# Turning the router matmul round: the 36 weight columns stationary, the 128 residual rows moving, in an encoder layer with hierarchical experts

## Chip, cores and metric

One core of one Trainium2 chip runs the whole kernel. The metric is the device time of one execution in microseconds (us); lower is better. Times given are a median of three executions, and one further execution was recorded by the profiler.

## What is computed

One encoder layer on 1024 tokens of width 1024: RMSNorm, one projection, three token mixers (neighbourhood attention, banded sliding-window attention, centred pooling), an output projection and a residual add; then RMSNorm and a hierarchical mixture of experts, a residual add and a final RMSNorm. What matters here is the router: for every token 4 group logits and 32 expert logits, the best group, and the two best experts in it.

```python
def hierarchical_moe(h, rg_w, rg_b, re_w, re_b, e_gate, e_up, e_down):
    t = h.reshape(-1, D)
    g_prob = softmax(t @ rg_w + rg_b)                 # 4 groups
    g_top_p, g_top = lax.top_k(g_prob, 1)
    e_logits = (t @ re_w + re_b).reshape(-1, 4, 8)    # 32 experts
    e_sel = jnp.take_along_axis(e_logits, g_top[:, :, None], axis=1)[:, 0]
    e_top_p, e_top = lax.top_k(softmax(e_sel), 2)
    ...
    for e in range(32):
        y = (silu(t @ e_gate[e]) * (t @ e_up[e])) @ e_down[e]
        out = out + combine[:, e:e + 1] * y
```

## The kernel before

Tokens are cut into TT = 8 tiles of 128 rows. Every engine has its own hand-written instruction list, and semaphores tie the lists together; nothing is reordered by a scheduler. The stages are: projection, mixers, the output projection in two halves of 512 output columns (its last matmul starts at 396.36 us), the router's end (to 411 us), 32 experts (to about 702 us), and the sum over experts with the final norm.

The large matmuls use a split of each fp32 operand into a high and a low part (three matmuls, lines 898 to 900 for the output projection). The router is the exception: its logits decide which expert a token goes to, so `logits(t)` (line 914) multiplies in full fp32. The program prints one instruction for such a matmul; the profile shows two records for it, and one record for a transposition.

The second half of the output projection, `out_proj(1, t)`, carries the router inside it. On TensorE a turn of the loop over t is: the first four k-steps of `out_proj(1, t)` (12 matmuls), the transposition of the second half of the previous tile's residual rows, `x1_transposes(t - 1, 1)`, that of the first half of this tile, `x1_transposes(t, 0)` (line 911), the other four k-steps, and `logits(t - 1)`: eight matmuls with the transposed residual rows `x1T` (128 x 128) stationary and the router weights `rw` (128 x 36) moving (line 925). The result, 128 tokens by 36 logits, lies in PSUM bank 6 or 7 in the form that VectorE wants.

```python
mm = nc.tensor.matmul(ps[:, 6 + t % 2, 0:NR], x1T[t % 2][:, k, :], rw[:, k, :],
                      start=(k == 0), stop=(k == KT - 1))
```

VectorE adds the residual (`residual`, line 1590), scales a tile's logits by the row's 1/rms (`take_logits`, line 1616, which waits for the logits and for `rstd_b`), writes the normalised rows (`normalise2`, line 1594), and copies the first half of the transposed rows from PSUM (`x1T_take`, line 1603). ScalarE sums the squares (`square2`, line 1256) and copies the second half (`x1T_copy`, line 1262); GpSimd makes 1/rms from the sum (line 1983). The ranks of tokens 0 to 511 within their experts are worked out while tiles 5 to 7 are still in the projection: `choose_group(0)`, `choose_first(0)`, `choose_second(0)` on VectorE (the last ends with line 1692), then `rank(0)` on TensorE (line 938).

After the last projection matmul comes the router's end. The logits of tile 6 are made in two halves round the transposition of tile 7's second half, then those of tile 7; VectorE takes them, chooses, ranks (line 938 again) and makes the lists of tokens (lines 956 and 1762); GpSimd gathers the first expert's rows (line 2085), and the experts start. `fill(n)` are matmuls without use that TensorE runs while it waits for VectorE.

In an expert's turn TensorE runs 36 large matmuls and ten transpositions; SyncE fetches the weights of expert e + 4 into the buffers that expert e gives back (`fetch_half`, line 596, waits for a count of TensorE's).

Of the kernel before, what the change touches and what calls it, by code (L numbers as in the profile page):

```python
# [26 lines left out]
F32 = mybir.dt.float32  # L27
# [5 lines left out]
P = 128  # L33
D = 1024
S = 1024
TT = S // P
KT = D // P
# [82 lines left out]
def encoder(nc, x, norm1_g, w_in, nat_tab, swa_sink, pool_w, pool_scale, w_out, norm2_g,  # L120
# [8 lines left out]
    with ExitStack() as ctx:  # L129
# [5 lines left out]
        def at(name, shape, dt, off):  # L135
            return nc.alloc_sbuf_tensor_at(name, shape, dt, offset=base + int(off))

        def sem(name):
            return ctx.enter_context(nc.semaphore(name))
# [111 lines left out]
        xThi = [at(f"xThi{i}", [P, KT, CAP], F32R, TMP + 2560 * i) for i in range(2)]  # L251
        xTlo = [at(f"xTlo{i}", [P, KT, CAP], F32R, (TMP + 5120, W + 53 * KB)[i]) for i in range(2)]
        sg = at("sg", [CAP, DE], F32, TD + 32 * KB)
        hx = at("hx", [COLS, DE], F32, TD + 33 * KB)
        hThi_e = at("hThi_e", [P, 2, CAP], F32R, TD + 34 * KB)
        hTlo_e = at("hTlo_e", [P, 2, CAP], F32R, TD + 34 * KB + 640)
# [71 lines left out]
        x1T_a = sem("x1T_a")  # L328
        x1T_b = sem("x1T_b")
        logit_mm = sem("logit_mm")  # L330
        logit_done = sem("logit_done")
        rd = sem("rd")
        chosen = sem("chosen")
# [362 lines left out]
        def _(pe):  # L696
# [217 lines left out]
            def logits(t, ks=range(KT)):  # L914

                if ks[0] == 0:
                    pe.wait_ge(x1T_a, t + 1)
                    if t >= 2:
                        pe.wait_ge(logit_done, t - 1)
                    if t == TT - 2:  # L920
                        pe.wait_ge(row_hots, 1)
                if ks[-1] >= 4:
                    pe.wait_ge(x1T_b, t + 1)
                for k in ks:
                    mm = nc.tensor.matmul(ps[:, 6 + t % 2, 0:NR], x1T[t % 2][:, k, :], rw[:, k, :],  # L925
                                          start=(k == 0), stop=(k == KT - 1))
                if ks[-1] == KT - 1:
                    mm.then_inc(logit_mm, 1)

            def rank(g):  # L930

# [30 lines left out]
                out_proj(0, t)  # L962
            pe.wait_ge(rw_scaled, 1)
            for t in range(TT):
                out_proj(1, t, range(4))
                if t >= 1:
                    x1_transposes(t - 1, 1)
                x1_transposes(t, 0)
                if t == TT - 2:
                    rank(0)  # L970
                out_proj(1, t, range(4, KT))
                if 1 <= t < TT - 1:
                    logits(t - 1)
            logits(TT - 2, range(4))
            x1_transposes(TT - 1, 1)
            logits(TT - 2, range(4, KT))
            logits(TT - 1)
            lists(0)
            pe.wait_ge(x1_done, 2 * TT)
            fill(FILL_CHOICE)  # L980
# [141 lines left out]
        def _(act):  # L1122
# [135 lines left out]
            def x1T_copy(t):  # L1258
                act.wait_ge(x1tr_b, t + 1)
                if t >= 2:  # L1260
                    act.wait_ge(logit_mm, t - 1)
                nc.scalar.copy(x1T[t % 2][:, 4:8, :], ps[:, 5, :].rearrange("p (c q) -> p c q", c=4)).then_inc(x1T_b, 1)

            for t in range(TT):
                square2(t)
                if t < TT - 1:
                    x1T_copy(t)

            act.wait_ge(rstd_b, TT)
            act.wait_ge(h2_end, 2)  # L1270
# [115 lines left out]
        def _(dve):  # L1386
# [224 lines left out]
                                        gbc[:].rearrange("q (p k) -> q k p", k=KT)[:, :, part], ALU.mult).then_inc(h2_end, 1)  # L1611

            def take_logits(t):
                dve.wait_ge(logit_mm, t + 1)
                dve.wait_ge(rstd_b, t + 1)
                nc.vector.scalar_tensor_tensor(out=logit[:, t, :], in0=ps[:, 6 + t % 2, 0:NR],
                                               scalar=stat[:, 3, t:t + 1], in1=rb[:], op0=ALU.mult, op1=ALU.add).then_inc(logit_done, 1)

            count = [0]
# [99 lines left out]
                v.tensor_reduce(ek[:, 2 * TG * g:2 * TG * (g + 1)], mine, AX_X, ALU.add)  # L1719

            nc.vector.memset(hx[:], 0.0).then_inc(zeroed, 1)
            dve.wait_ge(g_in, 32)
            for g in range(TT):
                residual(g)
# [469 lines left out]
```

## Time and profile before

| what | us |
|---|---|
| median of 3 executions | 737.96 (737.53 to 738.65) |
| the profiled execution, its own time | 738.25 |
| its span (first to last recorded instruction) | 736.4 |
| TensorE busy with matmuls | 707.0 (96%) |
| VectorE busy | 513.5 (70%) |
| ScalarE busy | 391.3 (53%) |
| GpSimd busy | 321.9 (44%) |
| granted TensorE clock, mean over the span | 0.996 of full speed |

The profile is of one execution. Its sections are: busy time of each engine, the span in 40 slices, DMA queues, the chain of work that ended last, and groups of instructions with what they waited for. PE is TensorE's matmuls, PEld its weight loads, DVE VectorE, ACT ScalarE, POOL GpSimd, SPq SyncE's DMA queue. The ends of matmuls are modelled, so the duration of one contains time in which the next already runs; distances between starts are measured.

### The profile page before, as it was taken

To read this page: it belongs to the slowest core of one execution; us is meant where nothing else is said; L and a number is where in the kernel's file an instruction comes from. 1 tells how busy PE (TensorE), PEld (TensorE's weight loads), DVE (VectorE), ACT (ScalarE), POOL (GpSimd) and SP (SyncE) were. 2 spreads that over 40 slices of the span, in tenths; PEclk is the share of its full clock that TensorE was granted. 3 is DMA by queue.
4 is the path that set the end of the run, shared out by engine and by line. 5 is a ranking of instruction groups with operands and counts; after the bars stand their busy time and mean duration, and the time that the engine had idled before them with its cause. 6 is when DMAs were issued, how large, how long until landed. Compare 5 with 4: busy or idle time off the path is not lost.

```text
span 736.4 us, 10256 instructions
## 1 busy us (share of the span) xinstructions
PE 707.0 (96%) x3757; PEld 510.2 (69%) x3757; DVE 513.5 (70%) x811; ACT 391.3 (53%) x585; POOL 321.9 (44%) x241
## 2 busy tenths in 40 slices
PE   7999999999999999999999899999999999999983
PEld 7888888886665445888889666666666666666631
DVE  5646422216887877513487888888888888888977
ACT  6500001104777778201123478888888888887815
POOL 1523458944677774440010254444444444442213
PEclk9999999999999999999999999999999999999998
DMA  9422112101400001905646499999999999999979
GB/s 305 139 58 58 30 56 58 29 0 36 109 1 1 1 1 38 289 17 201 225 160 251 139 335 387 391 384 380 382 388 383 390 387 385 383 383 381 399 270 357
DMA packets 62419, 157.74 MB, mean 214 GB/s; under 512 B 10168, under 2 KB 24992, under 8 KB 62368
## 3 DMA queue, kind: packets, MB, share of 16 engines
q1 hardware_dynamic: 55728, 139.58, 52.7%
q0 software_dynamic: 6336, 16.89, 6.8%
q8 instruction: 31, 0.51, 0.3%
q10 hardware_dynamic: 304, 0.59, 0.2%
q14 instruction: 20, 0.16, 0.1%
HBM read 142.36 MB, written 18.87 MB: 219 GB/s over the span
## 4 chain that ended last, share of the span: by engine, by line
PE 86%; DVE 5%; DMA 3%; issue 2%; ACT 2%; POOL 2%; DVEq 0%; SPq 0%; POOLq 0%
PE ps L1015 8%; PE ps L1020 8%; PE ps L1023 8%; PE ps L733 6%; PE ps L734 6%; PE ps L732 6%; PE ps L898 4%; PE ps L1046 4%; PE ps L1042 4%; PE ps L900 4%; PE ps L1050 4%; PE ps L899 4%; PE ps L836 3%; PE ps L991 2%; PE ps L925 2%
## 5 line engine op out<-in xcount | busy, mean ns | idle before, releaser
L1818 DVE TENSOR_TENSOR wgulo<-wgu,unit 128x2048 fp32r<-128x2048 f32 x64 | 146.3, 2287 | 26.1 <-ACT unit L1283 26.0
L1283 ACT CAST unit<-wgu 128x2048 fp32r<-128x2048 f32 x64 | 122.4, 1912 | 2.4 <-DVE eid L1779 1.1
L2092 POOL DMA_INDIRECT expert_rows<-ysb,idx x32 | 71.1, 2221 | 107.1 <-ACT ysb L1330 106.1
L2085 POOL DMA_INDIRECT xg<-h_rows,idx x32 | 59.1, 1847 | 71.6 <-PE ps L991 58.9
L732 PE MATMUL ps<-hThi,whi 128*128 128x512 f32 x200 | 78.3, 392 | 0.0
L734 PE MATMUL ps<-hThi,wlo 128*128 128x512 f32 x200 | 77.9, 389 | 0.0
L733 PE MATMUL ps<-hTlo,whi 128*128 128x512 f32 x200 | 77.8, 389 | 0.0
L1824 DVE TENSOR_TENSOR wdlo<-wd,unit 128x2048 fp32r<-128x2048 f32 x32 | 73.1, 2285 | 2.5 <-ACT unit L1292 2.5
L1015 PE MATMUL ps<-unit,xThi 128*80 128x512 f32 x256 | 70.8, 398 | 0.8 <-ACT xThi L1307 0.8
L1020 PE MATMUL ps<-unit,xTlo 128*80 128x512 f32 x256 | 69.2, 391 | 0.0
L1023 PE MATMUL ps<-wgulo,xThi 128*80 128x512 f32 x256 | 69.1, 391 | 0.0
L2047 POOL TENSOR_SCALAR pswa<-pswa,esum 128x384 f32<-128x384 f32 (+1 forms) x48 | 56.6, 1194 | 18.8 <-DVE esum L1540 18.8
L1292 ACT CAST unit<-wd 128x2048 fp32r<-128x2048 f32 x32 | 61.1, 1910 | 4.4 <-DMA wd<-in_expert_w_down 4.4
L1144 ACT COPY kb<-ps 64x512 f32<-64x512 f32 x8 | 4.7, 583 | 92.6 <-DVE ps L1417 92.5
L1020 PEld LDWEIGHTS ps<-unit,xTlo 128*80 128x80 f32 x256 | 37.8, 148 | 21.1 <-DVE xTlo L1831 0.2
L1023 PEld LDWEIGHTS ps<-wgulo,xThi 128*80 128x80 f32 x256 | 37.8, 148 | 21.1
L898 PE MATMUL ps<-wohi,oThi 128*128 128x512 f32 x128 | 51.3, 401 | 0.0
L900 PE MATMUL ps<-wohi,oTlo 128*128 128x512 f32 x128 | 50.0, 391 | 0.0
L899 PE MATMUL ps<-wolo,oThi 128*128 128x512 f32 x128 | 49.9, 390 | 0.0
L1184 ACT ACTIVATE pswa<-pswa,mneg 128x385 f32<-128x385 f32 (+1 forms) x64 | 37.5, 588 | 18.2 <-DVE mneg L1533 18.0
L1015 PEld LDWEIGHTS ps<-unit,xThi 128*80 128x80 f32 x256 | 35.4, 148 | 16.7 <-ACT xThi L1307 0.9
L1980 POOL TENSOR_SCALAR stat<-stat 128x1 f32<-128x1 f32 x16 | 5.5, 343 | 88.1 <-ACT h L1256 64.4
(226 smaller groups left out, 1453.4 us busy)
## 6 DMA issues: line engine op xcount, KB each, us to landing
wgu<-in_expert_w_gate SPq DMA_DIRECT2D x64, 512.0 KB, 13.0
wgu<-in_expert_w_up SPq DMA_DIRECT2D x64, 512.0 KB, 15.7
wd<-in_expert_w_down SPq DMA_DIRECT2D x32, 1024.0 KB, 18.0
y<-expert_rows SPq DMA_DIRECT2D x16, 512.0 KB, 10.4
wraw<-in_w_in SPq DMA_DIRECT2D x14, 512.0 KB, 3.9
xin<-in_x SPq DMA_DIRECT2D x8, 512.0 KB, 6.7
x<-in_x SPq DMA_DIRECT2D x8, 512.0 KB, 7.5
out<-fo SPq DMA_DIRECT2D x8, 512.0 KB, 3.8
```

The costliest lines, as they stand in the source:

```text
L732: nc.tensor.matmul(bank, whi[i % 2][:, k, :], hThi[:, k, cols], start=(k == 0), stop=False)
L733: nc.tensor.matmul(bank, whi[i % 2][:, k, :], hTlo[:, k, cols], start=False, stop=False)
L734: mm = nc.tensor.matmul(bank, wlo[i % 2][:, k, :], hThi[:, k, cols], start=False, stop=(k == KT - 1))
L898: nc.tensor.matmul(ps[:, g % 4, :], oThi[t][:, k, :], wohi[n][:, k, :], start=(k == 0), stop=False)
L899: nc.tensor.matmul(ps[:, g % 4, :], oThi[t][:, k, :], wolo[n][:, k, :], start=False, stop=False)
L900: mm = nc.tensor.matmul(ps[:, g % 4, :], oTlo[t][:, k, :], wohi[n][:, k, :], start=False, stop=(k == KT - 1))
L1015: nc.tensor.matmul(bank, xThi[e % 2][:, 4 * a + k, :], hi[:, :, k * DE:(k + 1) * DE], start=(a == 0 and k == 0), stop=False)
L1020: nc.tensor.matmul(bank, xTlo[e % 2][:, 4 * a + k, :], hi[:, :, k * DE:(k + 1) * DE], start=False, stop=False)
L1023: mm = nc.tensor.matmul(bank, xThi[e % 2][:, 4 * a + k, :], lo[:, :, k * DE:(k + 1) * DE], start=False, stop=(a == 1 and k == 3))
L1283: nc.scalar.copy(weight_unit(e, a)[:], raw_half(wgu, e, a)).then_inc(ahi_done, 1)
L1818: nc.vector.tensor_tensor(raw_half(wgulo, e, a), raw_half(wgu, e, a), weight_unit(e, a)[:].bitcast(F32), ALU.subtract).then_inc(alo_done, 1)
L1824: nc.vector.tensor_tensor(wdlo[e % RING][:].rearrange("p j d -> p (j d)").rearrange("p (a f) -> p a f", a=2), wd[e % RING][:].rearrange("p ...
```

## The change

The operands of the router matmul change places: `rw[:, k, :]` (36 columns) is stationary and `x1T` (128 columns) moves, so the product is 36 logits by 128 tokens, on 36 partitions. ScalarE copies it to a 128 x 128 buffer in SBUF, whose other 92 rows VectorE has set to zero once (`lt`, two buffers), and TensorE transposes that buffer back into columns 128 to 255 of the same PSUM bank, from which VectorE takes it. In the stream the transposition of tile t - 2 stands behind the first k-step of `out_proj(1, t)`. At the end the logits of tile 6 are no longer split round the transposition of tile 7's rows. Line numbers below are those of the changed kernel in the order listings; 898 to 900 became 902 to 904, 911 became 915, 925 became 929.

```diff
--- before.py
+++ after.py
@@ -251,6 +251,7 @@
         xThi = [at(f"xThi{i}", [P, KT, CAP], F32R, TMP + 2560 * i) for i in range(2)]
         xTlo = [at(f"xTlo{i}", [P, KT, CAP], F32R, (TMP + 5120, W + 53 * KB)[i]) for i in range(2)]
         sg = at("sg", [CAP, DE], F32, TD + 32 * KB)
+        lt = [at(f"lt{i}", [P, P], F32, TD + 32 * KB + 512 * i) for i in range(2)]
         hx = at("hx", [COLS, DE], F32, TD + 33 * KB)
         hThi_e = at("hThi_e", [P, 2, CAP], F32R, TD + 34 * KB)
         hTlo_e = at("hTlo_e", [P, 2, CAP], F32R, TD + 34 * KB + 640)
@@ -328,6 +329,9 @@
         x1T_a = sem("x1T_a")
         x1T_b = sem("x1T_b")
         logit_mm = sem("logit_mm")
+        lt_zeroed = sem("lt_zeroed")
+        lt_copied = sem("lt_copied")
+        logit_turned = sem("logit_turned")
         logit_done = sem("logit_done")
         rd = sem("rd")
         chosen = sem("chosen")
@@ -922,10 +926,15 @@
                 if ks[-1] >= 4:
                     pe.wait_ge(x1T_b, t + 1)
                 for k in ks:
-                    mm = nc.tensor.matmul(ps[:, 6 + t % 2, 0:NR], x1T[t % 2][:, k, :], rw[:, k, :],
+                    mm = nc.tensor.matmul(ps[0:NR, 6 + t % 2, 0:P], rw[:, k, :], x1T[t % 2][:, k, :],
                                           start=(k == 0), stop=(k == KT - 1))
                 if ks[-1] == KT - 1:
                     mm.then_inc(logit_mm, 1)
+
+            def logits_turned(t):
+
+                pe.wait_ge(lt_copied, t + 1)
+                nc.tensor.transpose(ps[:, 6 + t % 2, P:2 * P], lt[t % 2][:], ident[:]).then_inc(logit_turned, 1)
 
             def rank(g):
 
@@ -962,7 +971,10 @@
                 out_proj(0, t)
             pe.wait_ge(rw_scaled, 1)
             for t in range(TT):
-                out_proj(1, t, range(4))
+                out_proj(1, t, range(1))
+                if t >= 2:
+                    logits_turned(t - 2)
+                out_proj(1, t, range(1, 4))
                 if t >= 1:
                     x1_transposes(t - 1, 1)
                 x1_transposes(t, 0)
@@ -971,10 +983,11 @@
                 out_proj(1, t, range(4, KT))
                 if 1 <= t < TT - 1:
                     logits(t - 1)
-            logits(TT - 2, range(4))
+            logits(TT - 2)
             x1_transposes(TT - 1, 1)
-            logits(TT - 2, range(4, KT))
+            logits_turned(TT - 2)
             logits(TT - 1)
+            logits_turned(TT - 1)
             lists(0)
             pe.wait_ge(x1_done, 2 * TT)
             fill(FILL_CHOICE)
@@ -1261,10 +1274,21 @@
                     act.wait_ge(logit_mm, t - 1)
                 nc.scalar.copy(x1T[t % 2][:, 4:8, :], ps[:, 5, :].rearrange("p (c q) -> p c q", c=4)).then_inc(x1T_b, 1)
 
+            def lt_copy(t):
+                act.wait_ge(logit_mm, t + 1)
+                if t == 0:
+                    act.wait_ge(lt_zeroed, 2)
+                if t >= 2:
+                    act.wait_ge(logit_turned, t - 1)
+                nc.scalar.copy(lt[t % 2][0:NR, :], ps[0:NR, 6 + t % 2, 0:P]).then_inc(lt_copied, 1)
+
             for t in range(TT):
+                if t >= 1:
+                    lt_copy(t - 1)
                 square2(t)
                 if t < TT - 1:
                     x1T_copy(t)
+            lt_copy(TT - 1)
 
             act.wait_ge(rstd_b, TT)
             act.wait_ge(h2_end, 2)
@@ -1611,9 +1635,9 @@
                                         gbc[:].rearrange("q (p k) -> q k p", k=KT)[:, :, part], ALU.mult).then_inc(h2_end, 1)
 
             def take_logits(t):
-                dve.wait_ge(logit_mm, t + 1)
+                dve.wait_ge(logit_turned, t + 1)
                 dve.wait_ge(rstd_b, t + 1)
-                nc.vector.scalar_tensor_tensor(out=logit[:, t, :], in0=ps[:, 6 + t % 2, 0:NR],
+                nc.vector.scalar_tensor_tensor(out=logit[:, t, :], in0=ps[:, 6 + t % 2, P:P + NR],
                                                scalar=stat[:, 3, t:t + 1], in1=rb[:], op0=ALU.mult, op1=ALU.add).then_inc(logit_done, 1)
 
             count = [0]
@@ -1719,6 +1743,8 @@
                 v.tensor_reduce(ek[:, 2 * TG * g:2 * TG * (g + 1)], mine, AX_X, ALU.add)
 
             nc.vector.memset(hx[:], 0.0).then_inc(zeroed, 1)
+            for i in range(2):
+                nc.vector.memset(lt[i][:], 0.0).then_inc(lt_zeroed, 1)
             dve.wait_ge(g_in, 32)
             for g in range(TT):
                 residual(g)
```

The end of the router stage on TensorE, before (`ident,x` is the transposition of residual rows, `rw,x1T` the logits, `tile_hot,row_hot` the first lists):

```order
L900 MATMUL ps<-wohi_149,oTlo_147 128x512
L925 MATMUL ps<-rw,x1T_167 128x36 [waits row_hots,logit_done,x1T_a]
L925 MATMUL ps<-rw,x1T_167 128x36 x3
L911 MATMUL ps<-ident,x_164 128x128 [waits x1T_b,x1_done]
L911 MATMUL ps<-ident,x_164 128x128 x3
L925 MATMUL ps<-rw,x1T_167 128x36 [waits x1T_b]
L925 MATMUL ps<-rw,x1T_167 128x36 x3
L925 MATMUL ps<-rw,x1T_168 128x36 [waits x1T_b,logit_done,x1T_a]
L925 MATMUL ps<-rw,x1T_168 128x36 x7
L956 MATMUL ps<-tile_hot_175,row_hot_173 80x64 [waits row_hots]
```

and after the change (`ident,lt` is the transposition back):

```order
L902 MATMUL ps<-wohi_149,oThi_139 128x512
L903 MATMUL ps<-wolo_151,oThi_139 128x512
L904 MATMUL ps<-wohi_149,oTlo_147 128x512
L929 MATMUL ps<-x1T_167,rw 36x128 [waits row_hots,x1T_b,logit_done,x1T_a]
L929 MATMUL ps<-x1T_167,rw 36x128 x7
L915 MATMUL ps<-ident,x_164 128x128 [waits x1T_b,x1_done]
L915 MATMUL ps<-ident,x_164 128x128 x3
L937 MATMUL ps<-ident,lt_219 128x128 [waits lt_copied]
L929 MATMUL ps<-x1T_168,rw 36x128 [waits x1T_b,logit_done,x1T_a]
L929 MATMUL ps<-x1T_168,rw 36x128 x7
L937 MATMUL ps<-ident,lt_220 128x128 [waits lt_copied]
L965 MATMUL ps<-tile_hot_175,row_hot_173 80x64 [waits row_hots]
```

All eight matmuls of tile 6 now stand ahead of the transposition of tile 7's rows; one transposition back, which waits for ScalarE, stands between the two tiles' logits and one behind them.

In the stream, from the logits of tile 5 to the first k-steps of tile 7's projection, the changed TensorE list reads:

```order
L929 MATMUL ps<-x1T_168,rw 36x128 [waits x1T_b,logit_done,x1T_a]
L929 MATMUL ps<-x1T_168,rw 36x128 x7
L902 MATMUL ps<-wohi_149,oThi_139 128x512 [waits x1_done,pool_out,oTlo_done]
L903 MATMUL ps<-wolo_151,oThi_139 128x512
L904 MATMUL ps<-wohi_149,oTlo_147 128x512
L937 MATMUL ps<-ident,lt_220 128x128 [waits lt_copied]
L902 MATMUL ps<-wohi_149,oThi_139 128x512 [waits x1_done,pool_out,oTlo_done]
L903 MATMUL ps<-wolo_151,oThi_139 128x512
L904 MATMUL ps<-wohi_149,oTlo_147 128x512
```

One transposition is set behind the first three projection matmuls, and a second set of the projection's waits behind it.

ScalarE's list over tiles 6 and 7 now (`ACTIVATE` sums the squares of a tile, the last one with its junk output in `ps`):

```order
L1283 COPY lt_220<-ps 36x128 [waits logit_turned,logit_mm]
L1269 ACTIVATE h_165,stat<-x_164 128x1024 [waits h2_stored0,x1_done]
L1275 COPY x1T_167<-ps 128x512 [waits logit_mm,x1tr_b]
L1283 COPY lt_219<-ps 36x128 [waits logit_turned,logit_mm]
L1269 ACTIVATE ps,stat<-x_164 128x1024 [waits x1_done]
L1283 COPY lt_220<-ps 36x128 [waits logit_turned,logit_mm]
L1295 ACTIVATE h_166<-h_166,stat 128x1024 [waits h2_end,rstd_b]
```

The copy of a tile's logits stands ahead of the next tile's sum of squares, and the last copy ahead of the last scaling.

## Rows read from the trace of the kernel before

**Rows 1.** page, part 4: shares of the chain that ended last, by engine.

```profile
PE 86%; DVE 5%; DMA 3%; issue 2%; ACT 2%; POOL 2%; DVEq 0%; SPq 0%; POOLq 0%
```

**Rows 2.** busy time by stretch (us; records), granted clock, DMA share, GB/s.

```profile
337.00:396.40 59.40, 59.40 (x346) 51.48 (x344) 34.95 (x60) 12.05 (x21) 5.68 (x14) 1.00 0.59 214
...
440.00:700.00 260.00, 259.97 (x1329) 173.57 (x1328) 231.49 (x182) 217.13 (x203) 113.83 (x56) 1.00 1.03 385
```

**Rows 3.** who waited for whom on SyncE's DMA queue, 330 to 736 us.

```profile
SPq L596 <- PE ps L1023: 104.6, 47, 3.5
```

**Rows 4.** TensorE in order of time, one tile: start us, us, line, shapes, records.

```profile
388.18 0.39 PE L900 MATMUL ps<-wohi,oTlo 128*128 128x512 f32 x1
388.41 1.87 PE L925 MATMUL ps<-rw,x1T 128*128 128x36 f32 x16
...
390.43 0.39 PE L899 MATMUL ps<-wolo,oThi 128*128 128x512 f32 x1
...
392.97 1.03 PE L911 MATMUL ps<-ident,x 128*128 128x128 f32 x8
...
394.07 0.39 PE L899 MATMUL ps<-wolo,oThi 128*128 128x512 f32 x1
```

**Rows 5.** TensorE in order of time, two other full-precision groups.

```profile
215.85 1.09 PE L854 MATMUL ps<-ptna,vtok 128*64 128x128 f32 x16
...
409.44 1.36 PE L956 MATMUL ps<-tile_hot,row_hot 128*80 128x64 f32 x16 [0.92 <-DVE row_hot L1710]
```

**Rows 6.** groups of TensorE instructions by form: busy us, mean ns, idle before.

```profile
L866 PE MATMUL ps<-cu,pwd 128*128 128x512 f32 x8 | 3.7, 605 | 0.0
```

**Rows 7.** order of time, engines around tile 6's second half.

```profile
389.41 1.06 ACT L1256 ACTIVATE h<-x 128x1024 f32<-128x1024 f32 x1 [4.31 <-DVE x L1590]
...
390.94 0.57 POOL L1983 TENSOR_TENSOR stat<-stat,neg_half 128x1 f32<-128x1 f32 x1
...
392.13 2.19 DVE L1594 SCALAR_TENSOR_TENSOR h<-x,stat,gbc 128x1024 f32<-128x1024 f32 x1
```

**Rows 8.** order of time: VectorE's choice for tiles 0 to 3, TensorE's ranks.

```profile
381.23 0.26 DVE L1616 SCALAR_TENSOR_TENSOR logit<-ps,stat,rb 128x36 f32<-128x36 f32 x1 [0.29 <-PE ps L925]
...
382.73 0.29 DVE L1692 TENSOR_TENSOR rt<-rs 128x128 f32<-128x128 f32 x1
...
384.75 0.39 PE L938 MATMUL ps<-rt,ut 128*128 128x128 f32 x2
```

**Rows 9.** groups of ScalarE instructions by form, two small ones.

```profile
L1298 ACT ACTIVATE rs<-rs 128x32 f32<-128x32 f32 x1 | 0.2, 229 | 2.1 <-DVE rt L1692 2.1
...
L1315 ACT CAST hThi_e<-ps 128x160 fp32r<-128x160 f32 x2 | 0.6, 292 | 0.0
```

**Rows 10.** order of time, all engines, end of the router stage.

```profile
396.36 0.39 PE L900 MATMUL ps<-wohi,oTlo 128*128 128x512 f32 x1
...
396.59 0.97 PE L925 MATMUL ps<-rw,x1T 128*128 128x36 f32 x8
...
396.79 0.69 DVE L1590 TENSOR_TENSOR x<-ps,x 128x512 f32<-128x512 f32 x1 [0.74 <-PE ps L900]
...
397.52 1.03 ACT L1256 ACTIVATE ps<-x 128x1024 f32<-128x1024 f32 x1 [3.33 <-DVE x L1590]
...
397.54 0.66 PE L911 MATMUL ps<-ident,x 128*128 128x128 f32 x4
...
398.03 2.98 PE L925 MATMUL ps<-rw,x1T 128*128 128x36 f32 x24
...
398.23 0.69 DVE L1603 COPY x1T<-ps 128x512 f32<-128x512 f32 x1 [0.75 <-PE ps L911]
...
399.05 0.56 POOL L1983 TENSOR_TENSOR stat<-stat,neg_half 128x1 f32<-128x1 f32 x1
...
401.05 0.25 DVE L1616 SCALAR_TENSOR_TENSOR logit<-ps,stat,rb 128x36 f32<-128x36 f32 x1 [0.75 <-PE ps L925]
```

**Rows 11.** order of time: the token lists, then the first gather.

```profile
410.84 0.22 DVE L1762 TENSOR_SCALAR idx<-ps 80x64 int32<-80x64 f32 x1
```

## The prediction

> **What bounds the kernel now.** I read the chain that ended last first. TensorE carries 86% of it and VectorE 5% [rows 1], so an edit counts where it lengthens TensorE's list or one of the few places where TensorE waits for somebody. Then the stretches [rows 2]. While the router's logits are made inside the output projection (337 to 396 us), matmuls cover the whole time at a granted clock of 1.00, the 2.4 GHz level: there TensorE is the bound, and whatever its list gains or loses goes straight into the time. In the experts' stage (440 to 700 us) matmuls again cover everything, but the DMA engines are full too, with 385 GB/s. Who waits for whom decides there: SyncE's fetches wait 104.6 us in sum for TensorE's matmuls [rows 3], so the weights follow TensorE and a late start of the stage should be a late end. Between the two lies the router's end, from the last projection matmul at 396.36 to the first gather, ordered by a chain through TensorE and VectorE [rows 10, 11]. The change touches the stream and this end, so the forecast is two sums.
>
> **The matmuls themselves.** The cost of a group is the distance between projection matmuls on its two sides less that of one projection matmul. Ordinary distance: 388.41 - 388.18 = 0.23 us. For a tile's logits, 390.43 - 388.41 = 2.02 us, less 0.23, is 1.79 us for 16 records (eight matmuls of two), 0.112 each; for eight transpositions 394.07 - 392.97 = 1.10, less 0.23, is 0.87, 0.109 each, and the last record's own length is 1.03 - 7 x 0.109 = 0.27 [rows 4]. What sets 0.112 is the load of 128 stationary columns, not the 36 moving ones: a group with 80 stationary and 64 moving columns needs (1.36 - 0.27)/15 = 0.073 a record [rows 5]. From 128 to 80 columns that is 0.039 less, so 36 columns load in about 0.04, an estimate from these two groups. Then the 128 moving columns are the limit. Their price is not shown for this shape. From above it is the present 0.112. From below stands a group with 64 stationary and 128 moving columns, (1.09 - 0.27)/15 = 0.055 [rows 5]; but by `times_values` its heads alternate between the lower and the upper half of the output partitions. The group with 128 stationary and 512 moving columns does not alternate: (3.7 - 0.605)/7 = 0.44 a record, 0.11 for a quarter of the columns [rows 6]. The router's output lies on the same 36 partitions throughout, so I take the value of the rows that do not alternate, 0.109. A tile's logits then cost 16 x 0.109 = 1.75 us and save 0.04.
>
> The Trainium skill says otherwise at one place and the same at another. Its page "TensorE: Matmul & The Clock Gate", section "Back-to-back issue gap", gives an isolated gap of N/2.4 + 2.5 ns, 56 ns for 128 moving columns; by that the sum would be the fast rival's below, and the transpositions at 0.109 don't fit it. Its page "FP8 and Floating Point Precision", section "TensorE Precision Notes", says that true fp32 takes four passes through the array; four times 128 columns at 2.4 GHz are 213 ns a matmul, which agrees with two records of 0.109 and speaks against this change, because the passes now run over 128 columns instead of 36.
>
> **In the stream.** Six transpositions back (tiles 0 to 5) are new TensorE work at 0.11 each [rows 4]. With the 0.04 saved per tile, TensorE's stream grows by 6 x (0.11 - 0.04) = 0.42 us. Do they wait? ScalarE's copy can start when the last logit record has ended, 0.27 after its start; it moves 128 elements per partition, between 0.229 for 32 and 0.292 for 160 [rows 9], so I take 0.29. With two handovers of 0.04 it is ready 0.64 after the last record's start; three projection matmuls behind that record take the list to about 0.11 + 3 x 0.23 = 0.80. That fits by some 0.15. The extra semaphore waits of the cut projection call cost nothing as long as TensorE's queue runs ahead; without that cover they are six times some hundredths.
>
> Behind the copy on ScalarE's list stands the sum of squares of the next tile. It began at 389.41, and must now wait for the logits' end (390.29) and the copy: about 390.6, 1.2 later. GpSimd's root then ends at 391.51 + 1.2 = 392.7, and VectorE's normalisation, which began at 392.13, slips to 392.8 or so [rows 7]. VectorE had 0.74 idle before its last residual [rows 10]; this is what is late next, and it is covered. VectorE's logits of tile 4 come behind the turned tile, 381.23 becoming about 382.1, so the choice that ended at 382.73 + 0.29 = 383.02 ends at 383.9; TensorE's ranks that need it start at 384.75 [rows 8]. Nothing there stops TensorE. The two zeroings are two 128 x 128 writes (0.29 each, the row of that width in [rows 8]) on VectorE before the first residual, while TensorE is in the projection's first half; should that cover fail, 0.6 in all.
>
> **At the end.** Count from T, the start of the last projection matmul (396.36). Before, VectorE took tile 7's logits at 401.05, T + 4.69 [rows 10]. The order was: half of tile 6's logits, transposition of tile 7's rows as soon as the residual was added, then the second half of tile 6's logits while VectorE copied the rows out (398.23 to 398.92), then tile 7's logits without a gap (24 records in one row of 2.98). Now all of tile 6's logits come first: they start at T + 0.23 and take 1.75, to T + 1.98. The four transpositions take 0.66, to 2.64. VectorE's copy takes 0.03 + 0.69, to 3.36, with only one transposition back on TensorE meanwhile; tile 7's logits wait for it. 0.03, then 16 x 0.109 + 0.27 = 2.01 bring T + 5.40. ScalarE's copy, 0.03 + 0.29, to 5.72. The transposition back from idle: four took 0.66, so one takes 0.66 - 3 x 0.109 = 0.33, plus 0.04, to 6.09. VectorE's take begins at T + 6.13, 1.44 later than before. Of this about 0.7 is the lost cover of the rows' copy and 0.75 the turn itself. ScalarE's last sum of squares (397.52 before) now begins at about T + 2.4 + 0.42, or 399.2, and 1/rms, which was ready at 399.61, is there about 1.7 later, before it is wanted [rows 10]. The lists, fills and choice behind keep their order, so the delay passes to the lists' end at 410.84 and the first gather at 411.97 [rows 11].
>
> Sum: 0.42 + 1.44 = +1.86 us. Against the profiled execution's 738.25 that is 740.1; the median shown is 0.29 lower, so 739.8. Bounds: with the shortest copy (0.23) and turn (0.27), and no cost of the order beyond the copy itself, +1.2; with a bubble of 0.15 at each turn and the logits at 0.112, +3.1.
>
> **Rivals.**
> Faster: the moving columns go at the alternating group's rate, 0.055 a record [rows 5]. A tile's logits cost 0.87 instead of 1.79, the stream loses 6 x (0.92 - 0.11) = 4.9 us, and at the end tile 6's logits hide behind the residual: transpositions to T + 1.8, copy to 2.5, logits 1.15 to 3.7, turn 0.73 to 4.4, 0.3 earlier. Together -5.2, or 732.8. It decides as soon as a record is below about 0.095, where 128 records save over 1.9. Against it stand the transpositions and the 512-column group. Chance 0.10.
>
> No change: the experts' stage is held by the weights, DMA being full there [rows 2], and the late start is absorbed while fetches for the first experts are in flight; only the stream or less is left, 0 to +0.5, 738.2. Against it, SyncE waits for TensorE and not the reverse [rows 3]. Chance 0.20.
>
> Slower still: the margin of 0.15 at each turn is not there, because the turned tile's load cannot run ahead of its wait; six bubbles of 0.3 are 1.8 more, 741.6. Chance 0.17.
>
> **How the numbers follow.** My forecast, 739.8, has 0.53. The measurement can tell about 0.2%, 1.5 us, from no change, so "slower" begins at 739.4; of my forecast's share 0.10 lies below that (its lower bound is 739.2). Slower: 0.43 + 0.17 = 0.60. Same: 0.20 + 0.10 = 0.30. Faster: 0.10. The range leaves out the fast rival and the upper tail: 738.0 to 741.7.
>
> **What would show it.** The logit groups at 1.75 between their neighbours, with LDWEIGHTS short; VectorE's take of the last logits 1.9 us later on the clock; a wait of about 0.7 before tile 7's logits for VectorE's copy; the first gather at about 413.8, and the experts' end moved by as much. A logit group under 1.5 us makes the forecast wrong on one side; idle TensorE before each turned tile, on the other; an expert stage that is shorter than before would mean that the start was absorbed.

## The result, and the profile after

| | before | changed |
|---|---|---|
| median of 4 executions, us | 737.98 | 742.61 |
| ratio, with its 95% interval | | 1.0064 (1.0049 to 1.0078) |
| span of the profiled execution, us | 736.4 | 741.0 |
| TensorE busy, us | 707.0 | 710.1 |
| VectorE, ScalarE, GpSimd busy, us | 513.5, 391.3, 321.9 | 513.6, 392.5, 322.5 |

The change makes the kernel 4.6 us slower. I had forecast slower, by 1.9 us, with a range to 741.7; the measured time lies above it.

The page's chain that ended last, by engine, for the changed kernel (before: [rows 1]):

```profile
PE 83%; DVE 6%; DMA 5%; ACT 2%; issue 2%; POOL 1%; SPq 1%; DVEq 0%; POOLq 0%
```

TensorE has lost 3% of the span in this chain to VectorE and DMA. Three anchors tell where the time went. The output projection, both halves, runs from its first record (line 898, now 902) to T, the start of the last one: 290.7 to 396.36 before, 290.4 to 398.61 now, 105.66 and 108.17 us. VectorE takes tile 7's logits at T + 4.69 before, at T + 6.34 now. From that take to the token lists it is 9.79 us in both. So 2.51 us came in the stream and 1.65 at the end. The remaining 0.5 is a balance, mainly of 0.7 more in the experts' stage and 0.3 less ahead of the projection. It is treated below.

TensorE in order of time round the logits of tile 5, changed kernel (start us, us, line, shapes, records), which answers to [rows 4]:

```profile
390.02 0.39 PE L904 MATMUL ps<-wohi,oTlo 128*128 128x512 f32 x1
390.34 1.94 PE L929 MATMUL ps<-x1T,rw 128*36 128x128 f32 x16
...
392.55 0.40 PE L903 MATMUL ps<-wolo,oThi 128*128 128x512 f32 x1
392.79 0.39 PE L904 MATMUL ps<-wohi,oTlo 128*128 128x512 f32 x1
393.02 0.27 PE L937 MATMUL ps<-ident,lt 128*128 128x128 f32 x1
...
393.36 0.39 PE L903 MATMUL ps<-wolo,oThi 128*128 128x512 f32 x1
```

A seam, below, is a place where the shape of the stationary operand changes, from 128 columns to 36 or back. Read the distance from the last projection record ahead of the group to the second one behind it, and take off two ordinary distances, 0.46: 392.55 - 390.02 - 0.46 = 2.07 us. Before it was 390.43 - 388.18 - 0.46 = 1.79 [rows 4]; I had put 1.75. The logits of a tile became 0.28 dearer instead of 0.04 cheaper. The transposition back (line 937) costs 393.36 - 392.79 - 0.46 = 0.11, as forecast. Look at the start of the group: the first router record begins 0.32 behind the last projection record, where 0.23 is usual.

The view of line 929, its weight loads, and what they waited for:

```profile
L929 PEld LDWEIGHTS ps<-x1T,rw x128: 109/113/113, 346.5 to 403.9; 128*36 128x36 f32 x128
...
  issue: 3.4, 8
  DVE x1T L1627: 0.8, 1
```

A load of 36 columns now lasts 0.113 us instead of 0.19, so the loads are short, as said. But eight times, once for each group, they had stood idle with "issue" as the reason: nothing that the profile shows held them. Before, this line had no such wait. (One of the eight, at tile 7, falls together with the wait for VectorE; with 65 columns, below, only that one is left.) The 0.8 is the wait for VectorE's copy of tile 7's rows that I had put at 0.7.

All engines at the end of the router stage, changed kernel, which answers to [rows 10] and [rows 11]:

```profile
398.61 0.39 PE L904 MATMUL ps<-wohi,oTlo 128*128 128x512 f32 x1
...
398.93 1.94 PE L929 MATMUL ps<-x1T,rw 128*36 128x128 f32 x16
...
400.79 0.66 PE L915 MATMUL ps<-ident,x 128*128 128x128 f32 x4
400.90 0.26 ACT L1283 COPY lt<-ps 36x128 f32<-36x128 f32 x1 [4.46 <-PE ps L929]
...
401.49 0.69 DVE L1627 COPY x1T<-ps 128x512 f32<-128x512 f32 x1 [1.76 <-PE ps L915]
...
402.32 1.91 PE L929 MATMUL ps<-x1T,rw 128*36 128x128 f32 x16 [0.77 <-DVE x1T L1627]
...
404.27 0.26 ACT L1283 COPY lt<-ps 36x128 f32<-36x128 f32 x1 [2.06 <-PE ps L929]
...
404.58 0.33 PE L937 MATMUL ps<-ident,lt 128*128 128x128 f32 x1 [0.35 <-ACT lt L1283]
...
404.95 0.25 DVE L1640 SCALAR_TENSOR_TENSOR logit<-ps,stat,rb 128x36 f32<-128x36 f32 x1 [1.61 <-PE ps L937]
...
414.74 0.22 DVE L1788 TENSOR_SCALAR idx<-ps 80x64 int32<-80x64 f32 x1
```

Tile 6's logits at T + 0.32, transposition of tile 7's rows at T + 2.18, VectorE's copy to T + 3.57, tile 7's logits from T + 3.71 to T + 5.62, ScalarE's copy, the turn, VectorE's take. The order is the forecast one. The first group and its two seams put the transposition 0.20 behind the forecast T + 1.98. From VectorE's copy to tile 7's logits it is 0.14 instead of the 0.03 of my sum, so they start 0.32 late. And they last 1.91 us, where my sum had 16 x 0.109 + 0.27 = 2.01: one record too many, for by my own reading of such a group it is 15 x 0.109 + 0.27 = 1.91. So the take is 0.21 late. Two errors of 0.11 cancel in this, which was luck.

### The profile page after: what moved, and what is told of

The parts are those of the page before. It is cut to its first block, busy times and chain, and to the rows that moved or that the text cites. A ratio compares the mean times of both kernels' runs of the same rounds, so it can differ in the third digit from the quotient of the medians.

```text
span 741.0 us, 10299 instructions
## 1 busy us (share of the span) xinstructions
PE 710.1 (96%) x3765; PEld 509.0 (69%) x3765; DVE 513.6 (69%) x813; ACT 392.5 (53%) x593; POOL 322.5 (44%) x241
## 4 chain that ended last, share of the span: by engine, by line
PE 83%; DVE 6%; DMA 5%; ACT 2%; issue 2%; POOL 1%; SPq 1%; DVEq 0%; POOLq 0%
PE ps L1028 7%; PE ps L1033 7%; PE ps L1036 7%; PE ps L737 6%; PE ps L738 6%; PE ps L736 6%; PE ps L902 4%; PE ps L904 4%; PE ps L903 4%; PE ps L1059 4%; PE ps L1063 4%; PE ps L1055 4%; PE ps L840 3%; DMA wd<-in_expert_w_down 3%; PE ps L1004 2%; PE ps L929 2%
```

## The experiments

The theories that I set against each other after this profile: (A) TensorE loads a 36-column operand only when it has finished with 128-column ones, and the reverse; (B) the bubble belongs to the short load; (C) it belongs to which operand moves. The table has what came out. Each ratio is against executions of the kernel before that were taken together with that run; the other columns are from one profile each.

| run | ratio to before (95%) | stream, us | take of tile 7 | lists after the take |
|---|---|---|---|---|
| before | 1 | 105.66 | T + 4.69 | 9.79 |
| changed | 1.0064 (1.0049 to 1.0078) | 108.17 | T + 6.34 | 9.79 |
| w64 | 1.0047 (1.0030 to 1.0064) | 108.06 | T + 6.38 | 9.79 |
| w65 | 1.0029 (1.0018 to 1.0040) | 106.15 | T + 6.11 | 9.77 |
| tail_only | 1.0009 (0.9995 to 1.0022) | 105.66 | T + 5.43 | 9.78 |
| dummy36 | 1.0047 (1.0030 to 1.0064) | 109.58 | T + 4.69 | 10.02 |
| dummy80 | 1.0041 (1.0022 to 1.0060) | 107.32 | T + 5.09 | 11.24 |
| w65_split | 1.0030 (1.0019 to 1.0041) | 106.21 | T + 5.85 | 9.78 |
| halves | 0.9974 (0.9965 to 0.9984) | 103.62 | T + 4.77 | 9.79 |
| halves_b | 0.9986 (0.9975 to 0.9997) | 103.58 | T + 4.77 | 9.78 |
| halves_tail | 0.9985 (0.9973 to 0.9996) | 103.60 | T + 4.99 | 10.43 |
| halves_raw | 0.9976 (0.9963 to 0.9989) | 103.58 | T + 4.56 | 9.79 |
| after_b | 1.0061 (1.0048 to 1.0074) | 108.17 | T + 6.34 | 9.79 |

"Stream" runs from the first projection record to T, the take is VectorE's take of tile 7's logits, and the last column is the time from it to the token lists (before: line 1762).

**One column more.** In both kernels the router weights and the router bias behind them are one buffer `rww`, so that a stationary operand can be read wider than 36 columns; what the extra columns give lands on partitions that nobody reads.

```diff
-mm = nc.tensor.matmul(ps[0:NR, 6 + t % 2, 0:P], rw[:, k, :], x1T[t % 2][:, k, :],
+mm = nc.tensor.matmul(ps[0:64, 6 + t % 2, 0:P], rww[:, k * NR:k * NR + 64], x1T[t % 2][:, k, :],
```

> The changed kernel, but the stationary operand of a router matmul is 64 columns wide instead of 36 (the 28 extra columns are the next weights in SBUF; their products go to PSUM partitions that nobody reads). Theory A (between a stationary operand of at most 64 columns and one of more, TensorE does not load ahead: it finishes the one kind before it loads the other, about 0.32 us per group of logits on both sides together): as the changed kernel, 742.6 us (within 1), and from one projection record to the next across a group of logits 2.5 us, against 2.25 in the kernel before. Rival B (the bubble comes with how much the number of columns changes, or from the load being short): smaller than at 36, about 2.35 us, total 741 to 742. Rival C (it comes from which operand moves, whatever the width): 2.5 us, as A; the run with 65 columns tells them apart.

The same with 65 in place of 64:

> As before with 65 columns, one more. Theory A: 65 columns use the full width as the projection's 128 do, the weights are loaded ahead again, and a group of logits takes 16 x 0.109 = 1.75 us, so 2.0 us from projection record to projection record; six groups in the stream save 6 x 0.3 and the two at the end 0.3 to 0.5: 740.3 us (739.9 to 740.8). Rival B: no difference to 64 columns. Rival C: no difference either, 742.6 us.

TensorE in order of time round a group of logits, w64:

```profile
389.06 0.39 PE L905 MATMUL ps<-wohi,oTlo 128*128 128x512 f32 x1
389.38 1.96 PE L930 MATMUL ps<-x1T,rww 128*64 128x128 f32 x16
...
391.61 0.40 PE L904 MATMUL ps<-wolo,oThi 128*128 128x512 f32 x1
```

and w65:

```profile
388.21 0.40 PE L905 MATMUL ps<-wohi,oTlo 128*128 128x512 f32 x1
388.44 1.91 PE L930 MATMUL ps<-x1T,rww 128*65 128x128 f32 x16
...
390.42 0.40 PE L904 MATMUL ps<-wolo,oThi 128*128 128x512 f32 x1
```

With 64 columns the group costs 391.61 - 389.06 - 0.46 = 2.09 us, with 65 columns 390.42 - 388.21 - 0.46 = 1.75, the value of the prediction. One column more saves 0.34 us a group; the stream falls from 108.06 to 106.15, which is 0.49 above before where my sum had 0.42. The bubble is neither graded by the number of columns nor bound to the operand that moves: it comes between 64 and 65. The first weight load of each of these two groups (w64, then w65) shows what it is:

```profile
389.38 1.72 PEld L930 LDWEIGHTS ps<-x1T,rww 128*64 128x64 f32 x16 [0.35 <-issue]
```

```profile
388.21 1.90 PEld L930 LDWEIGHTS ps<-x1T,rww 128*65 128x65 f32 x16
```

With 65 columns it begins together with the last projection matmul, 0.23 ahead of its own matmul; with 64 it begins 0.32 behind that projection matmul, together with its own. At the end w65 takes tile 7's logits at T + 6.11 (prediction: T + 6.13).

**The order at the end alone.** The kernel before, with this edit:

```diff
-            logits(TT - 2, range(4))
+            logits(TT - 2)
             x1_transposes(TT - 1, 1)
-            logits(TT - 2, range(4, KT))
```

> The kernel before, with the changed kernel's order at the end alone: all eight logit matmuls of tile 6 ahead of the transposition of tile 7's rows. My prediction's term: VectorE takes tile 7's logits 0.7 us later (T + 5.4 instead of T + 4.7, T the start of the last projection record), total 738.7 us (738.4 to 739.0). Rival: the order costs nothing, since the residual of tile 7 is late anyhow: T + 4.8, 738.0 us.

```profile
396.43 0.39 PE L900 MATMUL ps<-wohi,oTlo 128*128 128x512 f32 x1
...
399.87 1.95 PE L925 MATMUL ps<-rw,x1T 128*128 128x36 f32 x16 [0.88 <-DVE x1T L1602]
...
401.85 0.26 DVE L1615 SCALAR_TENSOR_TENSOR logit<-ps,stat,rb 128x36 f32<-128x36 f32 x1 [0.97 <-PE ps L925]
```

(In order of time: T, tile 7's logits, VectorE's take of them.) The logits of tile 7 waited 0.88 for VectorE's copy, and the take came at T + 5.43, 0.74 later. The total, 1.0009 with an interval that holds 1, can't tell this from nothing; the trace can.

**A change of width by itself.** The kernel before, its router untouched, with seven useless matmuls in the projection's stream:

```diff
             for t in range(TT):
-                out_proj(1, t, range(4))
+                out_proj(1, t, range(2))
+                if t < TT - 1:
+                    if t >= 3:
+                        pe.wait_ge(logit_done, t - 2)
+                    nc.tensor.matmul(ps[0:36, 6 + (t + 1) % 2, 256:384], ident[:, 0:36], ones[:], start=True, stop=True)
+                out_proj(1, t, range(2, 4))
```

> The kernel before, with one useless full-precision matmul (36 stationary columns of the identity, 128 moving, two records) after the second k-step of the projection in tiles 0 to 6 of the second half. Theory A: each costs its two records, 0.22, plus the two changes of width, 0.3: 0.52 us, 7 x 0.52 = 3.6, total 741.6 us. Rivals B and C (bubble from the group of logits itself: its waits, its moving operand in fresh SBUF): 0.22 each, 739.5 us.

and with 80 in place of 36 in the added line:

> The kernel before with the same seven useless matmuls as in the run with 36 columns, but with 80 stationary columns. Theory A (the full width is used from 65 columns on, no change of width): 0.22 us each for two records, the projection 7 x 0.22 = 1.6 us longer, total 1.6 us above before. Rival (any extra matmul of another kind in the projection's stream costs 0.5): 3.9 us longer, as with 36 columns.

TensorE round one of them, dummy36:

```profile
366.85 0.40 PE L900 MATMUL ps<-wohi,oTlo 128*128 128x512 f32 x1
367.17 0.41 PE L969 MATMUL ps<-ones,ident 128*36 128x128 f32 x2
...
367.85 0.39 PE L899 MATMUL ps<-wolo,oThi 128*128 128x512 f32 x1
```

and dummy80:

```profile
366.21 0.39 PE L900 MATMUL ps<-wohi,oTlo 128*128 128x512 f32 x1
366.44 0.38 PE L969 MATMUL ps<-ones,ident 128*80 128x128 f32 x2
...
366.89 0.40 PE L899 MATMUL ps<-wolo,oThi 128*128 128x512 f32 x1
```

With 36 columns it costs 367.85 - 366.85 - 0.46 = 0.54 us, with 80 columns 366.89 - 366.21 - 0.46 = 0.22, its two records. The difference, 0.32, is the price of going from 128 columns to 36 and back, and it is the same for these two records as for a group of 16. The streams say the same: 3.92 and 1.66 longer, 0.56 and 0.24 each.

The total of dummy80 missed what I expected (1.6 us above before; it was about 3). Busy time by stretch, with the granted clock in the third column from the end, dummy80:

```profile
397.00:402.00 5.00, 4.94 (x40) 4.66 (x38) 2.63 (x4) 1.78 (x3) 0.77 (x2) 0.94 0.65 184
402.00:406.00 4.00, 4.00 (x26) 4.00 (x27) 3.12 (x18) 1.91 (x2) 0.00 (x0) 0.50 0.99 376
```

From 402 to 406 us, at the router's end, the clock was granted at 0.50, that is 1.2 GHz, and the lists came 11.24 us after the take instead of 9.79. The fall began before the take: the 24 logit records behind the last transposition lasted 3.39 us instead of 2.98, which is why the take came at T + 5.09 and not T + 4.69. It isn't the price of 80 columns, for in dummy36 the clock of the same stretch was 0.69, and the lists came 10.02 after the take. In the other profiles it was 1.00, but for halves_tail below. What pulled it down I can't say: in both runs matmul records follow each other without a gap there.

**What is left when the change of width is gone.** w65 with the old order at the end:

```diff
+            logits(TT - 2, range(4))
-            logits(TT - 2)
             x1_transposes(TT - 1, 1)
+            logits(TT - 2, range(4, KT))
             logits_turned(TT - 2)
             logits(TT - 1)
             logits_turned(TT - 1)
```

> The changed kernel with 65 stationary columns and with the old order at the end (half of tile 6's logits, transposition of tile 7's rows, the other half, tile 7's logits). What is left of the change is then the six transpositions back in the stream and the turn at the end. Theory: stream +0.5, and VectorE takes tile 7's logits at T + 5.4 instead of T + 6.1 and T + 4.7 before; total 1.2 us above before (0.9 to 1.6). Rival: VectorE's take of the last logits waits for the rows' 1/rms, which GpSimd has late because ScalarE's sum of squares stands behind the copy of tile 6's logits: then T + 5.4 to 6.0 and up to 1.8 above before.

```profile
399.50 0.33 PE L938 MATMUL ps<-ident,lt 128*128 128x128 f32 x1 [0.35 <-ACT lt L1285]
...
402.29 0.25 DVE L1642 SCALAR_TENSOR_TENSOR logit<-ps,stat,rww 128x36 f32<-128x36 f32 x1 [1.16 <-PE ps L938]
```

(the turn of tile 6, and VectorE's take of tile 7's logits.) The take came at T + 5.85, not T + 5.4: TensorE stood 0.35 us ahead of tile 6's turn, waiting for ScalarE's copy, and tile 7's logits stood behind it in the list. Neither my theory nor the rival (1/rms was ready before the take) had this wait. The total missed too: 0.3% above before, some 2.2 us, where I expected 1.2 (0.9 to 1.6).

**The two halves of the array at once.** If up to 64 columns use half of the array's width, two such matmuls can run side by side, as the attention's values do at 0.055 a record [rows 5]. The even k-steps of the router go to partitions 0 to 63, the odd ones to 64 to 127; the turn adds the halves.

```diff
-mm = nc.tensor.matmul(ps[0:NR, 6 + t % 2, 0:P], rw[:, k, :], x1T[t % 2][:, k, :],
-                      start=(k == 0), stop=(k == KT - 1))
+mm = nc.tensor.matmul(ps[64 * (k % 2):64 * (k % 2) + 64, 6 + t % 2, 0:P], rww[:, k * NR:k * NR + 64], x1T[t % 2][:, k, :],
+                      start=(k < 2), stop=(k >= KT - 2), skip_group_check=True)
...
-nc.tensor.transpose(ps[:, 6 + t % 2, P:2 * P], lt[t % 2][:], ident[:])
+nc.tensor.matmul(ps[:, 6 + t % 2, P:P + NR], lt[t % 2][:], stk[:], start=True, stop=True)
...
-nc.scalar.copy(lt[t % 2][0:NR, :], ps[0:NR, 6 + t % 2, 0:P])
+nc.scalar.copy(lt[t % 2][:], ps[:, 6 + t % 2, 0:P])
...
+nc.vector.tensor_tensor(stk[:], ident[:, 0:NR], ident[:, 64:64 + NR], ALU.add)
```

> The changed kernel, with the router's even k-steps into PSUM partitions 0 to 63 and the odd ones into 64 to 127 (64 stationary columns each), and one full-precision matmul against two stacked identities in place of the transposition back, which turns and adds the two halves. Theory (as with the attention's values, two records of different halves run at once, 0.109 a pair; changes of width cost 0.32 a group; the turn is two records, 0.22): a group of logits takes 0.87 + 0.32 instead of 1.79, the stream is 6 x (0.60 - 0.22) = 2.3 us shorter than before, VectorE takes tile 7's logits at T + 4.8; total 2.2 us below before. Rival (two halves do not overlap when both read the same kind of operand from 128 rows): 16 x 0.109 + 0.32, the stream 3 us longer than before, total 5 us above.

TensorE round a group of logits and a turn (line 941), halves:

```profile
385.15 0.39 PE L906 MATMUL ps<-wohi,oTlo 128*128 128x512 f32 x1
385.46 1.09 PE L931 MATMUL ps<-x1T,rww 128*64 128x128 f32 x16
...
386.83 0.40 PE L905 MATMUL ps<-wolo,oThi 128*128 128x512 f32 x1
387.06 0.40 PE L906 MATMUL ps<-wohi,oTlo 128*128 128x512 f32 x1
387.30 0.31 PE L941 MATMUL ps<-stk,lt 128*128 128x36 f32 x2
...
387.75 0.39 PE L905 MATMUL ps<-wolo,oThi 128*128 128x512 f32 x1
```

The 16 records last 1.09 us together, (1.09 - 0.27)/15 = 0.055 each; the group costs 386.83 - 385.15 - 0.46 = 1.22 with its two changes of width, the turn 387.75 - 387.06 - 0.46 = 0.23. The stream is 2.04 us shorter than before and the take at T + 4.77, both within 0.3 of the expectation. This version is faster than both kernels: 0.9974 of before (0.9965 to 0.9984). Repeated:

> The run halves again, on the chip of the other two: 2.2 us below before (1.3 to 2.9), T + 4.8, lists 9.8 us after the take.

0.9986 (0.9975 to 0.9997), with the same anchors. The gain is there both times, 1.9 and 1.0 us; the second is below the 1.3 at which my range began.

**Its end in another order.**

```diff
             logits(TT - 2)
             x1_transposes(TT - 1, 1)
+            logits(TT - 1, range(4))
+            logits(TT - 1, range(4, KT))
             logits_turned(TT - 2)
-            logits(TT - 1)
             logits_turned(TT - 1)
```

> The same, with another order at the end: tile 6's logits, transposition of tile 7's rows, the first half of tile 7's logits under VectorE's copy of the rows, the second half, then both turns. Theory: VectorE takes tile 7's logits at T + 4.4 to 4.5, 0.3 to 0.4 earlier than without it; total 2.5 us below before. Rival: the take is then held by 1/rms (square sum behind the copy of tile 6's logits), T + 4.7 or later and no gain over the run without it.

VectorE at the end, halves_tail (take of tile 6's logits, the last part of the raw rows, take of tile 7's):

```profile
396.95 0.26 DVE L1643 SCALAR_TENSOR_TENSOR logit<-ps,stat,rww 128x36 f32<-128x36 f32 x1 [1.09 <-PE ps L941]
397.13 1.08 DVE L1636 TENSOR_TENSOR h<-x,gbc 128x512 f32<-128x512 f32 x1
...
398.13 0.25 DVE L1643 SCALAR_TENSOR_TENSOR logit<-ps,stat,rww 128x36 f32<-128x36 f32 x1
```

The take of tile 7's logits stood behind a 1.08 us instruction of VectorE's own, and came at T + 4.99: a miss, with a cause that I had not listed. And the lists came 10.43 behind it. In total the run is 1.1 us below before, not 2.5. Busy time by stretch:

```profile
401.50:403.30 1.80, 0.00 (x0) 0.00 (x0) 1.59 (x11) 0.35 (x2) 0.00 (x0) 1.00 0.70 275
403.30:405.50 2.20, 2.18 (x12) 2.19 (x13) 1.26 (x5) 0.23 (x1) 0.00 (x0) 0.61 0.05 19
```

TensorE had no work for 1.8 us (no record in the first stretch), and its clock fell to 0.61 as a mean of the next. The last run moves that VectorE instruction ahead of the two takes:

```diff
             x1T_take(TT - 1, 1)
-            take_logits(TT - 2)
             last_raw(1)
+            take_logits(TT - 2)
             take_logits(TT - 1)
```

> The run halves_tail, with VectorE's last part of the raw rows (1.08 us) moved ahead of its take of tile 6's logits, into the time in which it waited. Theory: the take of tile 7's logits no longer stands behind it and comes at T + 4.3 instead of T + 5.0, the choice is ready 0.7 earlier, TensorE's idle stretch ahead of the ranks shrinks from 1.8 to 1.1 us, its clock stays at the full level, and the lists come 9.8 us after the take instead of 10.4; total 2.6 us below before. Rival: the drop of the granted clock in that stretch has nothing to do with the idle time; then the lists stay 10.4 us after the take and the total is at most 2.0 below before.

```profile
398.38 0.56 POOL L2011 TENSOR_TENSOR stat<-stat,neg_half 128x1 f32<-128x1 f32 x1
...
399.04 0.25 DVE L1643 SCALAR_TENSOR_TENSOR logit<-ps,stat,rww 128x36 f32<-128x36 f32 x1 [0.49 <-POOL stat L2011]
```

(GpSimd's root, VectorE's take.) TensorE's stretch without a record shrank from 1.84 to 1.41 us, the clock stayed at 1.00 and the lists came 9.79 behind the take again. One profile each shows the idle stretch and the clock going together; dummy36 and dummy80 show that the clock can fall without one. The take itself came at T + 4.56, not T + 4.3: 1/rms of tile 7 was ready only at 398.94, T + 4.47, and VectorE took at once. In halves_tail it was ready at T + 3.72, with ScalarE's list in the same order, so this is not the rival of halves_tail (the square sum behind the copy) but came with the move itself:

```profile
397.12 1.09 DVE L1636 TENSOR_TENSOR h<-x,gbc 128x512 f32<-128x512 f32 x1
...
397.33 0.96 POOL L2008 TENSOR_SCALAR stat<-stat 128x1 f32<-128x1 f32 x1 [6.95 <-ACT ps L1274]
```

GpSimd's step ahead of the root lasted 0.96 us and ended 0.08 behind VectorE's instruction; in halves_tail, where that one came later, it lasted 0.22. The total is 0.9976 (0.9963 to 0.9989), no better than halves within the intervals.

**The changed kernel again.**

> The changed kernel again, on the chip of the other two: projection 2.5 us longer than before, take at T + 6.3; total 4.2 us above before (3.7 to 5.0). If the 0.7 us that its experts' stage was longer in the first profile was no chance, the stage is again 288.7 us or more against 288.1.

It repeats to 0.01 us in the stream and at the end, and 1.0061 in total. Its experts' stage, from the first gate record to the last down record, was 289.5 us, after 288.8 in the first profile and 288.1 in that of before (there from 417.5 to 705.6, so somewhat later than the 702 given above). By the mark that I had set (288.7 or more) that is no chance. But this stage, whose code none of the edits touches, lies between 288.0 (tail_only) and 289.5 over all profiles; 288.2 in w64, which has the whole change in it, and 289.1 in dummy80, which has none of it. So my mark could not decide it, and whether the longer stage, and with it the last 0.5 us of the 4.6, is chance or effect stays open.

## Why the prediction was wrong, point by point

**The step that failed** is the price of a tile's logits: "A tile's logits then cost 16 x 0.109 = 1.75 us and save 0.04." The record's price was right to the last digit (w65 gives exactly 1.75), and so was the choice between the rows for it: the slow one of [rows 6], not the alternating one. What failed was to put the group between its neighbours with nothing at the seams. A 36-column operand next to 128-column ones costs 0.32 us at its two seams, shown by w64 against w65 and by dummy36 against dummy80. Six groups are 1.9 us of the stream's 2.51, and the two seams of tile 6's group put the end 0.20 behind the forecast. The Trainium skill has the rule that I did not weigh: its page "TensorEngine Tiling (Array Packing)", section "Key Properties", says that a change of tiling mode, not of the tile alone, drains TensorE. The same page of the Trainium skill lists tiles of 64 and 32 columns beside the full width in its section "Available Configurations". The step between 64 and 65 columns agrees with it. Neither the page nor my rows had a price.

The trace of before could have given one. TensorE in the attention, a group with 64 stationary columns between transpositions with 128:

```profile
208.40 0.65 PE L836 MATMUL ps<-ident,pna 128*128 128x128 f32 x4
208.99 1.09 PE L854 MATMUL ps<-ptna,vtok 128*64 128x128 f32 x16
210.01 0.66 PE L836 MATMUL ps<-ident,pna 128*128 128x128 f32 x4
```

Four transpositions take 0.59 us to the next group, where 4 x 0.109 is 0.44; sixteen records take 1.02, where 16 x 0.055 is 0.88. That leaves 0.15 and 0.14, about 0.3 for the two seams, an estimate from these lines. This form of group [rows 5] carried both a low price and this toll, and I had only discussed the price.

The idle time of weight loads, with "issue" as the reason, is a poorer guide. Between 200 and 290 us line 836 has 9.2 us of it in 21 waits, but 7.6 of them stand behind line 821, whose operands have 128 columns and 64 rows; only 5 waits of 0.17 stand behind 64 columns. Line 860 has 7.0 us in 24 waits, and 20 of these, 5.7 us, lie inside its own groups, where each short load waits out matmuls of 512 moving columns and no shape changes.

**The transposition back in the stream**, 0.11 each: right (0.11). With it and w65 the sum of the stream, 0.42, measured 0.49.

**Do they wait for ScalarE's copy?** No wait was forecast and none is in the stream. The six bubbles of my third rival are not there; its number, 741.6, was nearer to the result than my own, but for another reason.

**VectorE and the square sums.** ScalarE's waiting behind the logits delayed 1/rms, as said, and nothing on TensorE stood for it. It was ready at T + 5.45, 2.2 later from T than before, where my sum gives 1.3 (1.7 on the clock). The other 0.9 is GpSimd's step ahead of the root: it began at 402.30, under VectorE's instruction of 402.26 (line 1633), and lasted 1.13 us instead of 0.22. In the eight profiles in which the two overlap at this place, GpSimd's step ended 0.08 or 0.09 behind VectorE's; in the other five it lasted 0.22. The root still came ahead of the take here.

**The end**: 1.44 later forecast, 1.65 measured. Of it 0.74 is the order of the list (tail_only; I had 0.7), the turn is 404.95 - 404.23 = 0.72 from the end of the logits to the take, against 0.75, and the rest is the 0.20 of the seams. My sum also had 0.11 too little for the handover from VectorE's copy and 0.11 too much for one record; that they cancel is luck. The old order alone does not bring the cover back: from w65 to w65_split the take gained 0.26 of the 0.74, because the turn of tile 6 waited for ScalarE.

**The experts' stage follows**: right. The first gather moved by 3.9 us (411.97 to 415.87) and the end by 4.6; the rival of absorption is refuted.

**The fast rival** was wrong for this change and right as a mechanism: 0.055 a record is to be had, but only if the list alternates between the halves. I had worked out its price and not asked what edit would earn it; that edit is the version that beats both kernels.

## What to carry to other kernels

Price a group of matmuls with its seams: where its stationary operand has up to 64 columns (measured at 36 and 64) and its neighbours have 128, TensorE did not load ahead, and 0.32 us per visit was far more than the 0.04 that the turned operands saved. Either widen the small operand to 65 columns or more with columns that nobody reads, or earn the toll by letting two halves run at once. A trace can price the seams before any edit is made: take the distance between starts across such a group and subtract what its records cost by themselves. Waits of weight loads for "issue" are a hint only; they also stand inside groups of one shape.

## What the runs showed of the hardware that I had not expected

- The width limit is sharp: 2.09 us for a group at 64 stationary columns, 1.75 at 65, at equal moving columns.
- Two full-precision matmuls with 64 stationary columns over all 128 rows, one to each half of the output partitions, run at 0.055 us a record against 0.109, also when the even and the odd steps of one sum over k are split between the halves.
- The granted clock fell to the 1.2 GHz level at the router's end for part of the time in three of the profiles: in halves_tail behind 1.8 us without a TensorE record, in dummy36 and dummy80 with matmul records end to end. It cost 0.6, 0.2 and 1.5 us between the take and the lists, and in dummy80 another 0.4 ahead of the take. What pulled it down in the last two is open. In the kernel before, with 1.1 us without a record there, it stayed at 1.00, and in halves_raw with 1.4.
- A small GpSimd instruction (128x1) took up to 1.14 us (halves) instead of 0.22 (before, halves_tail) when VectorE's instruction with operands of 128x512 ran, 1.08 us long, and it ended 0.08 or 0.09 behind that one, in all eight profiles where the two overlap at the router's end.
